# Products without a use in TensorE's waits, and several small moves around them, in a two-block transformer kernel

## The reference, cut to what matters

```python
mod = silu(c) @ w_ada[i] + b_ada[i]              # 6 x 1024 numbers, layer by layer
h = rms_norm(x) * (1 + scale) + shift            # before each part
q, kv, q_i, k_i, w_i, p_shift, ga, gr = split(xn @ w_in)      # second block
mixed = p_shift + (prev - p_shift) * mu          # r, k, v, wl, al, gl
w = -softplus(-(w0 + tanh(wl) @ w2)) - 0.5 ; g = sigmoid(gl) @ g2
...
g_sel = argmax(xt @ wg_router)                   # one of 4 groups
e_in  = (xt @ we_router + e_bias) of that group  # 8 experts of it
top 2 of e_in -> weights w_top, experts          # 32 experts in all
out = sum over experts of w * (silu(xt @ wg) * (xt @ wu)) @ wd
```

## Time and profile before

| | us |
|---|---|
| median of 3 runs | 2029.95 |
| lowest and highest | 2028.24, 2035.53 |
| the profiled execution | 2033.85 |
| its span, first to last instruction | 2032.2 |
| mean granted clock of TensorE | 0.983 of full |

### The profile page before, as it was taken

How to read it: one execution, slowest core, us unless ns; L and a number is a source line. 1 busy time by engine, 2 the same in 40 slices (tenths; PEclk the granted TensorE clock), 3 DMA queues, 4 the chain that set the end, 5 groups by cost and what they waited for, 6 DMA issues and landing times.

```text
span 2032.2 us, 25520 instructions
## 1 busy us (share of the span) xinstructions
PE 1953.3 (96%) x10686; PEld 1320.9 (65%) x10686; DVE 841.0 (41%) x1402; ACT 281.9 (14%) x602; POOL 290.2 (14%) x258
## 2 busy tenths in 40 slices
PE   6999999999999999989999999999997999999998
PEld 3444458888878874457888888768786554455444
DVE  2566338888884345192533213774324100000001
ACT  2000020000000121163000011241202100000000
POOL 0001115555632220000111010400000000000000
PEclk9999999999999999999999999989997999999999
DMA  9545204554441350004976460321026999999997
GB/s 400 196 165 180 69 21 156 161 163 163 161 176 57 147 247 0 0 1 154 397 264 210 156 253 21 145 89 35 14 96 248 408 430 428 428 429 428 428 428 317
DMA packets 48781, 420.22 MB, mean 207 GB/s; under 512 B 5440, under 2 KB 5456, under 8 KB 22960
## 3 DMA queue, kind: packets, MB, share of 16 engines
q1 hardware_dynamic: 29376, 344.73, 41.8%
q0 software_dynamic: 18880, 71.18, 10.6%
q10 hardware_dynamic: 432, 2.96, 0.4%
HBM read 417.81 MB, written 1.05 MB: 206 GB/s over the span
## 4 chain that ended last, share of the span: by engine, by line
PE 82%; DVE 7%; DMA 6%; issue 2%; ACT 1%; DVEq 0%; ACTq 0%; SPq 0%
PE PS L1269 9%; PE PS L1399 8%; PE PS L1034 8%; PE PS L1001 7%; PE PS L1044 6%; PE PS L1110 5%; DMA ring<-w_moe 5%; PE PS L1454 4%; PE PS L1420 4%; PE PS L1257 4%; PE PS L1095 4%; DVE SC L1793 3%; PE PS L1130 3%; PE PS L1433 3%; PE PS L1227 2%
## 5 line engine op out<-in xcount | busy, mean ns | idle before, releaser
L1269 PE MATMUL PS<-ring,A 128*64 128x512 f32 x1024 | 223.5, 593 | 3.7 <-DMA ring<-w_moe 2.9
L1269 PEld LDWEIGHTS PS<-ring,A 128*64 128x64 f32 x1024 | 73.9, 137 | 150.1 <-issue 141.7
L1793 DVE SCALAR_TENSOR_TENSOR SC<-A,CS,SC 128x512 f32<-128x512 f32 x208 | 164.8, 847 | 9.5 <-DMA A<-ada 7.7
L1399 PE MATMUL PS<-A,ring 128*128 128x512 f32 x368 | 159.7, 594 | 0.0
L1034 PE MATMUL PS<-A,ring 128*128 128x256 f32 x704 | 156.3, 383 | 1.2 <-ACT A L593 1.2
L1001 PE MATMUL PS<-ring 128*128 128x256 f32 x672 | 150.9, 380 | 0.0
L1034 PEld LDWEIGHTS PS<-A,ring 128*128 128x128 f32 x704 | 134.1, 192 | 23.4 <-issue 5.2
L1001 PEld LDWEIGHTS PS<-ring 128*128 128x128 f32 x672 | 126.9, 190 | 24.6 <-issue 7.7
L1399 PEld LDWEIGHTS PS<-A,ring 128*128 128x128 f32 x368 | 69.4, 190 | 89.8 <-issue 89.8
L446 POOL DMA_DIRECT2D ring<-ada x64 | 35.0, 547 | 562.7 <-DVE SC L1793 346.7
L1257 PE MATMUL PS<-ring,A 128*64 128x512 f32 x512 | 113.4, 595 | 0.7 <-ACT A L692 0.7
(11 more groups left out here) (360 smaller groups left out, 2518.2 us busy)
## 6 DMA issues: line engine op xcount, KB each, us to landing
ring<-w_moe SPq DMA_DIRECT2D x96, 2048.0 KB, 18.4
ring<-w_fin SPq DMA_DIRECT2D x44, 1024.0 KB, 7.1
ring<-ada POOLq DMA_DIRECT2D x64, 512.0 KB, 4.4
A<-ada POOLq DMA_DIRECT2D x64, 512.0 KB, 4.6
ring<-w_fout SPq DMA_DIRECT2D x16, 1408.0 KB, 7.2
ring<-w_conv SPq DMA_DIRECT2D x8, 1536.0 KB, 13.5
ring<-w_qkv SPq DMA_DIRECT2D x6, 2048.0 KB, 15.9
ring<-w_win SPq DMA_DIRECT2D x6, 2048.0 KB, 10.4
```

The costliest lines, as they stand in the source:

```text
L1269: mm = pe.matmul(PS[CAP * e:CAP * (e + 1), g, :], XG[:, k * P + e * CAP:k * P + (e + 1) * CAP], slot("moe", k // 2, w, w + 512), start=(k ...
L1399: mm = pe.matmul(PS[:, 3 * (j % 2) + c, :], slot("conv", j, k * 384 + c * 128, k * 384 + c * 128 + 128), h_of(k, 512), start=(k == 0), sto ...
L1793: ins = dve.scalar_tensor_tensor(out=ACC[:, i, :], in0=w, scalar=scale, in1=ACC[:, i, :], op0=ALU.mult, op1=ALU.add)
```

## The change

Eleven small edits:

1. `keep_on(bank, n)` is new: n products of the identity with 256 columns of constants, into a PSUM bank that nobody reads. 14 stand before the first product of the kernel, 7 after the router's transposes, 3 after the rank products.
2. The load of `lora` gets a semaphore of its own (`landed8`).
3. GpSimd's token shift runs in five groups of three tiles.
4. ScalarE takes Sigmoid and Tanh of the shifted tiles between two copies of the input projection, ahead of the attention; an early preload of the Exp table goes, a preload of the Sigmoid table stands after the attention.
5. `GATE_CUTS`: the 16 gate products in the attention stand as 5, 4, 2, 1, 1, 1, 1, 1 in place of 2 in each pair.
6. In `ffn_out_folded`, `ada_sum(1, 9)` moves ahead of the wait for the last hidden piece, and the wait for `folded` 113 moves one product down.
7. The router's product is turned round: 8 products with 36 output rows and 256 tokens, each issued as soon as its piece of the norm is there. VectorE copies the 36 rows, TensorE transposes them back (2 transposes, after the first 4 token transposes).
8. `first_max` has one instruction less: the constant `iota` holds its values minus 99.
9. The bias is added after the group has been found; `g_shift` and `e_diff` come after the indicator.
10. VectorE makes the first placement columns (two instructions of L2049) right after the count, ahead of the mixing weights and of the branch.
11. The dense path's waits are counted for this; it is not run here.

```diff
-LANDED = {"cout": 8, "fin0": 4}
+LANDED = {"cout": 8, "fin0": 4, "lora": 8}
+GATE_CUTS = (0, 5, 9, 11, 12, 13, 14, 15, 16)
-            for g in range(3):
-                a, b = 5 * g, 5 * g + 5
+            for g in range(5):
+                a, b = 3 * g, 3 * g + 3
...
-            table(ACT.Exp)
...
                 win_copy(i, (i + 2) % 4)
+                if i == 19:
+                    act.wait_ge(sem("mixed"), 5)
+                    act.activation(RP[:, 256:768], RP[:, 256:768], ACT.Sigmoid).then_inc(sem("lora_in"), 1)
+                    act.activation(RP[0:64, 0:256], RP[0:64, 0:256], ACT.Tanh).then_inc(sem("lora_in"), 1)
             dsa_attention()
...
-            act.wait_ge(sem("mixed"), 5)
-            act.activation(RP[0:64, 0:256], RP[0:64, 0:256], ACT.Tanh).then_inc(sem("lora_in"), 1)
-            act.activation(RP[:, 256:768], RP[:, 256:768], ACT.Sigmoid).then_inc(sem("lora_in"), 1)
+            table(ACT.Sigmoid)
...
+            def keep_on(bank, n):
+                for i in range(n):
+                    pe.matmul(PS[:, bank, 0:256], ident, C[:, 0:256], start=True, stop=True)
...
                     if i == 0:
+                        ada_sum(1, 9)
                         pe.wait_ge(sem("hid_done"), 24)
                     fold(b + 1, 1, w0[:, 11:22], HID4[:, 11:22, 1, :])
-                    if i == 0:
-                        ada_sum(1, 9)
...
-                        pe.wait_ge(sem("folded"), 113)
+                        pe.wait_ge(sem("folded"), 111)
                     fold(b + 1, 0, FS[1], FT[1]).then_inc(sem("product"), 1)
                     slot_landed(pe, "fout0", 2 * i + 1)
+                    if i == 0:
+                        pe.wait_ge(sem("folded"), 113)
...
-                    gate_part(0, 7, 2 * p, 2 * p + 2)
+                    gate_part(0, 7, GATE_CUTS[p], GATE_CUTS[p + 1])
...
             pe.wait_ge(sem("zeros"), 2)
+            keep_on(5, 14)
             ada_first(0)
...
             for k in range(KD):
                 h_wait(5, k)
-            pe.wait_ge(sem("root_done"), 6)
-            for t in range(2):
-                for k in range(KD):
-                    mm = pe.matmul(PS[:, 6, t * 64:t * 64 + 36], XN[:, k * SEQ + t * P:k * SEQ + (t + 1) * P],
-                                   vec("router", k * 36, k * 36 + 36), start=(k == 0), stop=(k == KD - 1))
+                mm = pe.matmul(PS[0:36, 6, 0:SEQ], vec("router", k * 36, k * 36 + 36), XN[:, k * SEQ:(k + 1) * SEQ],
+                               start=(k == 0), stop=(k == KD - 1))
...
+            keep_on(4, 7)
             pe.wait_ge(sem("indicated"), 1)
...
+            keep_on(4, 3)
             busiest = count_of(pe)
...
-                link(dve.tensor_scalar(dst, dst, -99.0, 99.0, ALU.mult, ALU.add))
-                link(dve.tensor_tensor(dst, dst, con("iota", 0, w).unsqueeze(1).to_broadcast([P, 2, w]), ALU.add))
+                link(dve.tensor_tensor(dst, dst, con("iota", 0, w).unsqueeze(1).to_broadcast([P, 2, w]), ALU.mult))
...
             dve.tensor_reduce(FLAG[:, :], PS[:, 6, 2 * NE:3 * NE], AX.X, ALU.max).then_inc(sem("counted"), 1)
+            dve.wait_ge(sem("place"), 1)
+            for t in range(2):
+                places(t, 0, EG)
             dve.wait_ge(sem("g_exp"), 1)
```

More of the change, by code:

```diff
@@ L288, in build @@
         LG = A[:, 5376:5504].rearrange("p (t e) -> p t e", t=2)
+        LT = A[0:36, 6656:6912]
         ST3 = A[:, 15360:16896].rearrange("p (b t) -> p b t", b=3)
@@ L1724, in _ @@
                 h_wait(5, k)
-            pe.wait_ge(sem("root_done"), 6)
-            for t in range(2):
-                for k in range(KD):
-                    mm = pe.matmul(PS[:, 6, t * 64:t * 64 + 36], XN[:, k * SEQ + t * P:k * SEQ + (t + 1) * P],
-                                   vec("router", k * 36, k * 36 + 36), start=(k == 0), stop=(k == KD - 1))
+                mm = pe.matmul(PS[0:36, 6, 0:SEQ], vec("router", k * 36, k * 36 + 36), XN[:, k * SEQ:(k + 1) * SEQ],
+                               start=(k == 0), stop=(k == KD - 1))
             mm.then_inc(sem("logits"), 1)
             for b in range(4):
+                if b == 1:
+                    pe.wait_ge(sem("logits_copied"), 1)
+                    for t in range(2):
+                        mm = pe.transpose(PS[:, 5, t * 64:t * 64 + 36], LT[:, t * P:(t + 1) * P], ident[0:36, 0:36])
+                    mm.then_inc(sem("logits"), 1)
                 for c in range(4):
@@ L2044, in add_output, with places @@
                     sem("y_out"), 1)
-            def dve_gathered():
-                def places(t, a, b):
-                    dve.tensor_tensor(PG[:, t, a * CAP:b * CAP].rearrange("p (e s) -> p e s", s=CAP),
-                                      IOTA64.unsqueeze(1).to_broadcast([P, b - a, CAP]),
-                                      RANK[:, t, a:b].unsqueeze(2).to_broadcast([P, b - a, CAP]),
-                                      ALU.is_equal).then_inc(sem("place"), 1)
+            def places(t, a, b):
+                dve.tensor_tensor(PG[:, t, a * CAP:b * CAP].rearrange("p (e s) -> p e s", s=CAP),
+                                  IOTA64.unsqueeze(1).to_broadcast([P, b - a, CAP]),
+                                  RANK[:, t, a:b].unsqueeze(2).to_broadcast([P, b - a, CAP]),
+                                  ALU.is_equal).then_inc(sem("place"), 1)
+            def dve_gathered():
                 def turn(it, first=False, last=False):
@@ L2065, in turn @@
                     dve.tensor_copy(YS[:, 512:1024], PS[:, 3, :]).then_inc(sem("ys_dve"), 1)
-                dve.wait_ge(sem("place"), 1)
-                for t in range(2):
-                    places(t, 0, EG)
                 for t in range(2):
@@ L2101, in dve_dense @@
                                 sem("place"), 1)
-                            dve.wait_ge(sem("place"), it * 8 + (4 * e + q + 2))
+                            dve.wait_ge(sem("place"), it * 8 + (4 * e + q + 4))
                             dve.tensor_tensor(HM[:, e * 1024 + q * 256:e * 1024 + q * 256 + 256], sg, PS[:, q, 256:512],
@@ L2202, in _ @@
             dve.wait_ge(sem("pv_dsa"), HEADS2)
-            dve.wait_ge(sem("mixed"), 15)
+            dve.wait_ge(sem("mixed"), 25)
             for m in range(4):
@@ L2342, in _ @@
             dve.wait_ge(sem("logits"), 1)
-            link(dve.tensor_copy(LG[:, :, 0:36], PS[:, 6, 0:128].rearrange("p (t e) -> p t e", t=2)[:, :, 0:36]))
-            G, E = LG[:, :, 0:4], LG[:, :, 4:36]
-            link(dve.tensor_tensor(E, E, vec("e_bias").unsqueeze(1).to_broadcast([P, 2, NE]), ALU.add))
+            dve.tensor_copy(LT, PS[0:36, 6, 0:SEQ]).then_inc(sem("logits_copied"), 1)
+            dve.wait_ge(sem("logits"), 2)
+            LP = PS[:, 5, 0:128].rearrange("p (t e) -> p t e", t=2)
+            G, E = LP[:, :, 0:4], LG[:, :, 4:36]
             small = RT[:, 8:32]
@@ L2366, in _ @@
             first_max(G, 4, 1, goh)
-            dve.tensor_tensor(gexp, G, wide(1, 4), ALU.subtract).then_inc(sem("g_shift"), 1)
+            link(dve.tensor_tensor(E, LP[:, :, 4:36], vec("e_bias").unsqueeze(1).to_broadcast([P, 2, NE]), ALU.add))
             link(dve.tensor_scalar(goh, goh, -NEG, NEG, ALU.mult, ALU.add))
@@ L2374, in _ @@
             first_max(E, NE, 3, oh[2])
+            dve.tensor_tensor(IND, oh[1], oh[2], ALU.add).then_inc(sem("indicated"), 1)
+            dve.tensor_tensor(gexp, G, wide(1, 4), ALU.subtract).then_inc(sem("g_shift"), 1)
             dve.tensor_tensor(two(0), two(3), two(2), ALU.subtract).then_inc(sem("e_diff"), 1)
-            dve.tensor_tensor(IND, oh[1], oh[2], ALU.add).then_inc(sem("indicated"), 1)
             dve.wait_ge(sem("ranked"), 1)
@@ L2445, in host_consts @@
     put("row", np.broadcast_to(np.arange(23.0) == 11, (P, 23)) * 1.0)
-    put("iota", np.broadcast_to(np.arange(32.0), (P, 32)))
+    put("iota", np.broadcast_to(np.arange(32.0) - 99.0, (P, 32)))
     put("eps", np.broadcast_to(np.array([EPS, GN_EPS, EPS * HD]), (P, 3)))
```

2 lines of the change are left out of this document (1 added, 1 removed).

## The result

The changed kernel takes **2013.91 us** (median of 4 runs, 2009.83 to 2015.62), the kernel before took 2030.18 beside it (4 runs, 2028.24 to 2035.53). The ratio is 0.9914, 95% interval 0.9893 to 0.9934: 16 us, 0.9%. The profiled execution took 2015.62, its span 2014.0, against 2033.85 and 2032.2 before; mean granted clock 0.991 against 0.983.

What follows compares the result with a forecast made beforehand. TensorE's chain to turn 0, then the stream of experts' weights, bounds the kernel. 0 - 2.6 - 3.0 - 4.5 - 8.7 = -18.8 us gives 2015 from the profile, 2011 from the median; forecast 2013, 8 in 10 between 2005 and 2021.

Steps and rivals of the forecast that it cites:

- The frame: End of the kernel: it moves as much as turn 0, the first expert turn, up to about 10 us.
- Rival 3: Expert weights: an unmoved part of their stream sets the end, not turn 0; 2024 us and up, chance 0.07.
- rival 4: Expert weights: the stream runs slower; at 5% less rate the kernel takes 2034 us, chance 0.03.
- the sum of -18.8: Whole kernel: beginning 0, feed-forward -2.6, sparse attention -3.0, mixer's start -4.5 and router -8.7 us added up.
- The beginning, 0: Kernel start: 14 products speed slot 0 by some 3 us, which is waited for at slot 3; 0 us.
- The bound on the other side: Kernel start: +3 us if the clock falls in the new waits and slot 3's 3.4 us take twice as long.
- The feed-forward, -2.6: Feed-forward: small product moves into a wait, -0.95 us, and the clock holds, -1.7; bounds -0.9 and -2.7.
- The sparse attention, -3.0: Sparse attention: smaller GpSimd groups and moved gate products shorten waits and hold the clock; -3.0 us, bounds -0.5 and -4.4.
- The mixer's start, -4.5: After the attention: earlier `lora` load saves 1.8 us of wait, held clock 2.7; bounds -1.8 and -5.3.
- The router, -8.7: Router: logits behind the pieces, shorter search and held clock bring turn 0 from 1567.86 to 1559.1; -8.7 us.
- Rival 2: Router: with the clock low throughout, products without a use delay TensorE; gain 1.4 to 3 us, 2019 us, chance 0.15.
- Rival 1: Feed-forward, attention, mixer: the clock falls anyway in the filled waits; 6.1 us missing, 2019 us, chance 0.13.

Runs made afterwards that it cites:

- experiment 1: The changed kernel without its 14 products ahead of the kernel's first product: 2012.3 us, ratio 0.9897 to the kernel before.
- 8: The changed kernel run again with no edit, in the second group of runs: 2011.80 us, ratio 0.9895 to the kernel before.
- experiment 12: The changed kernel with two gate products in each attention pair again, GpSimd's five groups kept: 2013.83 us, ratio 0.9913 to the kernel before.
- experiment 3: The changed kernel with products without a use added around the spreading in norms 1 to 5: 2011.56 us, ratio 0.9896 to the kernel before.
- experiment 11: The changed kernel with 14 and 6 products in the router in place of 7 and 3: 2016.69 us, ratio 0.9924 to the kernel before.
- Experiments 4: The kernel before with the router's edits alone: 2022.64 us, ratio 0.9951 to the kernel before.
- 7: The changed kernel with the feed-forward's small product and `folded` wait where they were before: 2012.3 us, ratio 0.9898 to the kernel before.
- experiments 6: The changed kernel with three GpSimd groups of five tiles and two gate products per attention pair again: 2012.74 us, ratio 0.9904 to the kernel before.
- Experiment 5: The changed kernel with the `lora` load, Sigmoid and Tanh where they were before: 2017.68 us, ratio 0.9924 to the kernel before.
- experiment 9: The changed kernel without its 14 starting products, with fills in the norms, first attention and mixer waits: 2006.08 us, ratio 0.9877 to the kernel before.

## Why the prediction was right, and where its reasons were not

**The frame held.** The end hangs on turn 0: it moved by 18.69, the last turn by 18.28, the span by 18.2. Rival 3 is refuted. So is rival 4: the last loads take 25.49 and 25.78 us, against 25.49 before. The forecast, 2013, was 0.9 us off the median, the sum of -18.8 within 0.6 of the profiled -18.2. Part of that is luck: two stretches that I didn't count (-1.65 at L982, +1.70 at 279.3) cancel, and the time of one execution moves by 6 us. The 17 us that I made of the sum for a median execution are less well confirmed than the 18.8, since the medians of the three comparisons are 16.3, 21.8 and 19.4 us apart. I put about 9 of the 18.8 to the clock; with 27.3 us less at the low clock it can be up to 13.7.

**The beginning, 0.** Right, and for the reason given: with the products slot 0 takes 3.17, and slots 2 and 3 are waited for; without them (experiment 1) it takes 5.80, and nothing is waited for. Two limits. I called the 6.11 of the earlier trace rows the low clock, but the profile grants 1.00 in that stretch, before as in experiment 1; why slot 0 is slow there isn't shown. And with the products it was 3.17 in nine profiles of ten, but 4.87 in 8. The bound on the other side showed itself in experiment 12: the clock fell behind the wait for slot 2 (from 28.77), and L990 began at 42.85. L990 was partly slow again, 8.36 us; it was 9.86 without the products, but 9.93 in experiments 3 and 11, which have them, so they don't decide it.

**The feed-forward, -2.6.** The size was right (-2.85), a step wrong. I put 1.7 of it to the clock that holds when half the wait is filled. Experiments 4 and 7 have the high clock with the old order, and the stage still takes 141.34 and 141.32: what follows waits for VectorE's product into `folded` 113 instead. Both edits are needed, in the other order of rank than I gave them. The relaxed wait lets TensorE go on with a part that is ready: by itself it takes away the wait of 1.42 and some tenths of hand-over, which I work out to 1.9 (not run alone). The small product in the wait adds its 0.95, but only with the relaxed wait, since VectorE's product ends at the same distance from the stage's start in either kernel (19.0 us). I had the relaxed wait as what lets the gain of the clock through; it is the gain. The low clock of this execution merely hid the wait in the earlier trace rows.

**The sparse attention, -3.0.** Measured -2.23. The clock held through the stage, as predicted, and L1999 never took over 2 us. What meeting GpSimd costs VectorE's scalings fell by 0.7 (0.5 predicted), and TensorE's wait for them from 3.7 to 2.2; "below 2 in all" missed by 0.2. Of my two sums, 4.35 with TensorE as the bound and 2.6 with VectorE, the measured one is near the second. The gain is largely by the cuts (experiments 6 and 12).

**The mixer's start, -4.5.** Measured -5.00: the wait 2.32 to 0.62, and 3.30 of the clock where I took 2.7 of 3.4. Experiment 5 undoes it and pays it back, in profile and time. The 3.30 aren't certain in each execution: in experiment 3's profile, with these edits, the clock fell and the stage took 30.24.

**The router, -8.7.** Measured -8.84, and nearly step by step, the times of after shifted by the 9.85 us that norm 5 comes earlier: logits end 1545.94 (1545.3 predicted), search 1546.81 (1546.3), rank products 1.3 (1.3), gather 1554.48 (1554.5) and 3.81 long (3.6), turn 0 1559.02 (1559.1). The clock came back at 1545.29.

**Rival 2, the products in the way,** was a matter of their number: at seven and three they end 0.38 and 0.16 before they are in the way, at fourteen and six they cost 3.25 (experiment 11). Its condition, a clock still low at 1549, didn't arise in any profile with the products in the router.

**Rival 1, the clock falls anyway,** is half true. In the feed-forward, the attention and the mixer's start it fell in one profile of those with their edits (experiment 3, mixer's start). Elsewhere, at the norms above all, it falls in most profiles and not in the same places, and the time spreads with it: the 33 executions of the kernel before go from 2027.81 us at a granted clock of 0.988 to 2037.66 at 0.982. In experiment 9 the fills removed most of the stretches and the spread together. The fills in norms 1 to 5 alone didn't (experiment 3, 6.1 us of spread); which of the others did it isn't separated.

On transposes, the runs of the change add nothing: in the changed kernel the clock rises at 1535.44, inside L1735, before the first transpose. Against the sentence of the Trainium skill ("TensorE: Matmul & The Clock Gate", Part 4) that transpose mode doesn't count as busy, there are only the earlier trace rows, one trace.

What remains open: the time alone doesn't tell the groups, the cuts, the feed-forward's order or the 14 products from nothing; their sizes are those of the profiles.

## What to carry to other kernels

Find first what the end hangs on; here it was the first use of a full ring of weights, and each microsecond won on TensorE's way to it was one at the end. Products without a use can pay in short waits for another engine, where the profile shows the clock falling and much TensorE work follows. Ahead of a transfer that comes at its own time they pay nothing (experiment 1), and more of them than the wait holds cost their own time (experiment 11). When the same kernel's executions lie 6 us apart, judge small edits by a table of stages over several profiles, and ask at an edit that "restores the clock" what is late next if the clock is high.

## What the runs showed of the hardware

TensorE's clock can fall with no idle gap right ahead of it. In experiment 9 the window before the fall and that after it:

```profile
1225.00:1228.15 3.15, 3.15 (x27) 3.03 (x25) 1.56 (x1) 0.75 (x2) 0.00 (x0) 1.00 0.00 0
1228.15:1234.98 6.83, 6.83 (x24) 5.93 (x24) 0.67 (x2) 0.18 (x1) 0.00 (x0) 0.51 0.01 2
```

TensorE is busy in all of it, and the clock goes from 2.4 to 1.2 GHz within this group, whose products are 8 columns wide:

```profile
1225.88 4.69 PE L1519 MATMUL PS<-V,A 128*128 128x8 f32 x32
```

Thirteen of the fourteen profiles have a low stretch that begins at this group; only experiment 3's hasn't, where the same 32 records take 3.63 us. I had counted on waits alone. That it is the form of these products that lets the clock fall isn't tested; no run changes them. (The Trainium skill, "TensorE: Matmul & The Clock Gate", section on oscillation, explains the falls in its kernel by waits for transfers; here there is none ahead.)

The other surprise is that which stretches are low changes between executions of one kernel: the clock is low at 279.3 in one of the changed kernel's three profiles and in no other kernel's, and at norm 5 it is low for 6.8, 6.8 and 3.4 us. (The same page of the Trainium skill, Part 1, says that the number of slow products at a kernel's start differs between runs of one kernel; here the first slot's 14 records took 3.17, 4.87 and 3.17 us in those three profiles, and the middle differs too.)
